# Moving a small gate product and its vector and scalar work from the middle of a projection stage to its beginning

## The reference, cut to what matters

```python
IN_SPLITS = (2 * MLSTM_HEADS * MLSTM_DQK, MLSTM_WIDTH, MLSTM_WIDTH,
    MLSTM_HEADS, MLSTM_HEADS,      # input gate, forget gate: 4 columns each
    3 * MOBA_WIDTH, MLA_Q_LORA, MLA_KV_LORA, MLA_ROPE)
...
hl = rms_norm_2(causal_block_attention(lq, lk, lv), g_mla_out)
...
mix = jnp.concatenate([hm.reshape(B, S, MLSTM_WIDTH), ha.reshape(B, S, MOBA_WIDTH),
                       hl.reshape(B, S, MLA_WIDTH)], axis=-1)
x = x + mix @ w_out
h2 = rms_norm_2(x, g_mlp_norm)
x = x + jnp.square(jax.nn.relu(h2 @ w_up)) @ w_down
```

## Time and profile before

| | us |
|---|---|
| median of 3 runs | 2105.74 |
| lowest, highest | 2096.07, 2106.62 |
| the profiled execution | 2099.57 |
| its span | 2097.4 |
| mean granted TensorE clock, share of full | 0.953 |

### The profile page before, as it was taken

How to read it: one execution, slowest core, us unless ns; L and a number is a source line. 1 busy time by engine, 2 the same in 40 slices (tenths; PEclk the granted TensorE clock), 3 DMA queues, 4 the chain that set the end, 5 groups by cost and what they waited for, 6 DMA issues and landing times.

```text
span 2097.4 us, 44494 instructions
## 1 busy us (share of the span) xinstructions
PE 1899.1 (91%) x16350; PEld 1789.6 (85%) x16350; DVE 1310.8 (62%) x1997; ACT 1145.0 (55%) x1929; POOL 960.3 (46%) x686
## 2 busy tenths in 40 slices
PE   7898788999999898788999999988799999889999
PEld 6787677999999887677999998966699998669999
DVE  2467866268943366775258973477687545768764
ACT  4644245457755655245456665664655456565544
POOL 4672017938997683015846988571200036402000
PEclk9999699999999999789999999997999999879999
DMA  5442003656665442003565665431266654204665
GB/s 191 127 126 72 1 2 113 181 149 181 186 192 168 141 131 72 21 2 96 165 173 158 186 185 157 136 100 41 81 173 198 187 165 121 76 26 142 187 192 174
DMA packets 146201, 271.51 MB, mean 129 GB/s; under 512 B 16225, under 2 KB 16482, under 8 KB 145762
## 3 DMA queue, kind: packets, MB, share of 16 engines
q1 hardware_dynamic: 144720, 265.29, 43.8%
q10 hardware_dynamic: 1298, 3.66, 0.5%
HBM read 267.84 MB, written 1.05 MB: 128 GB/s over the span
## 4 chain that ended last, share of the span: by engine, by line
PE 66%; DVE 15%; ACT 10%; POOL 5%; issue 3%; DMA 0%; ACTq 0%; DVEq 0%; SPq 0%
PE bank L655 65%; ACT arena L1281 7%; POOL ring_split L643 5%; ACT hi_ring L1281 1%; PE bank L762 1%; DVE arena L1813 1%; DVE arena L1812 1%; DVE arena L2121 1%; DVE small L2120 1%; ACT L1281 1%; DVE u L1883 1%; DVE arena L2256 0%; DMA arena<-in_masks 0%; DVE arena L2363 0%; DVE arena L2250 0%
## 5 line engine op out<-in xcount | busy, mean ns | idle before, releaser
L643 POOL TENSOR_TENSOR ring_split<-ring,hi_ring 128x512 fp32r<-128x512 f32 x682 | 960.1, 1432 | 954.5 <-ACT hi_ring L1281 943.8
L1281 ACT ACTIVATE hi_ring<-ring 128x512 fp32r<-128x512 f32 x1002 | 618.0, 630 | 519.1 <-PE bank L655 496.8
L655 PE MATMUL bank<-u_hi,hi_ring 128*128 128x256 f32 (+1 forms) x2480 | 677.5, 286 | 58.8 <-POOL ring_split L643 45.2
L655 PE MATMUL bank<-u_split,hi_ring 128*128 128x256 f32 (+1 forms) x2480 | 666.1, 281 | 0.4 <-DVE u_split L1888 0.2
L655 PE MATMUL bank<-u_hi,ring_split 128*128 128x256 f32 (+1 forms) x2480 | 666.0, 281 | 0.0
L655 PEld LDWEIGHTS bank<-u_hi,hi_ring 128*128 128x128 f32 (+1 forms) x2480 | 453.5, 188 | 73.5 <-POOL ring_split L643 51.2
L655 PEld LDWEIGHTS bank<-u_split,hi_ring 128*128 128x128 f32 (+1 forms) x2480 | 453.5, 188 | 2.7 <-DVE u_split L1888 1.0
L655 PEld LDWEIGHTS bank<-u_hi,ring_split 128*128 128x128 f32 (+1 forms) x2480 | 453.6, 188 | 1.1
L655 PE MATMUL bank<-arena 64*64 64x64 f32 (+6 forms) x3680 | 261.9, 268 | 52.6 <-ACT arena L1281 13.4
L655 PEld LDWEIGHTS bank<-arena 64*64 64x64 f32 (+3 forms) x3680 | 227.0, 165 | 93.9 <-issue 53.3
L1921 DVE TENSOR_TENSOR ring_split<-ring,hi_ring 128x512 fp32r<-128x512 f32 x320 | 215.4, 694 | 116.2 <-ACT hi_ring L1281 112.6
(11 more groups left out here) (246 smaller groups left out, 2390.0 us busy)
## 6 DMA issues: line engine op xcount, KB each, us to landing
ring<-in_stream SPq DMA_DIRECT2D x1002, 256.0 KB, 2.7
par<-in_params ACTq DMA_DIRECT2D x4, 637.0 KB, 4.9
cst<-in_cst SPq DMA_DIRECT2D x1, 1058.0 KB
h<-in_x SPq DMA_DIRECT2D x1, 1024.0 KB
out<-h ACTq DMA_DIRECT2D x3, 256.0 KB, 2.7
arena<-in_masks SPq DMA_DIRECT2D x1, 416.0 KB
out<-h ACTq DMA_DIRECT2D x2, 128.0 KB, 2.1
arena<-in_positions ACTq DMA_DIRECT2D x1, 1.0 KB
```

Source lines behind the costliest of these rows:

```text
L643: nc.gpsimd.tensor_tensor(ring_lo[:, c, :], ring[:, c, :], hi_ring[:, q % HI_RING, :].bitcast(F32), ALU.subtract).then_inc(lo_by_pool, 1)
L655: ins = nc.tensor.matmul(o, l, r, start=start, stop=stop)
L1281: return nc.scalar.activation(o, i, f, **kw)
```

## The change

The group `if` goes to the place right behind `kpe` in the bank order, in the weight stream, and in TensorE's program. On ScalarE its Abs, Exp, table load and Ln go behind the square of the latents, ahead of `aq`; a second table load, back to `natural_log_exp_and_others`, is added behind the Ln. On VectorE all ten operations go ahead of the latents' norm. The request `hi.upto("if", 0)` ahead of the root "latent qk" becomes `hi.upto("uv")`. What is computed is the same.

```diff
--- before.py
+++ after.py
@@ -101,8 +101,8 @@
 for i in range(len(MERGE)):
     SIZES1 += [(m[0], 16) for m in MERGE[i + 1:i + 2]] + [(MERGE[i][1], 8)]
 SIZES1 += [("WO", 64), ("U first", 16), ("U second", 16)] + [(f"U{i}", 16) for i in range(2, 22)] + [("D", 176)]
-SIZES2 = [("cq first", 16), ("cq second", 16), ("cq1", 8), ("kpe", 8)] + [(n, 16) for n in ("aq", "ak", "av", "qk0", "qk1")]
-SIZES2 += [("uq0", 6), ("uq1", 6), ("uk0", 2), ("uk1", 2), ("uv", 4), ("if", 8), ("mv0", 32), ("mo0", 16), ("mo1", 16)]
+SIZES2 = [("cq first", 16), ("cq second", 16), ("cq1", 8), ("kpe", 8), ("if", 8)] + [(n, 16) for n in ("aq", "ak", "av", "qk0", "qk1")]
+SIZES2 += [("uq0", 6), ("uq1", 6), ("uk0", 2), ("uk1", 2), ("uv", 4), ("mv0", 32), ("mo0", 16), ("mo1", 16)]
 SIZES2 += [("WO attention", 32), ("WO", 32), ("U first", 16), ("U second", 16)] + [(f"U{i}", 16) for i in range(2, 16)] + [("D", 256)]
 assert sum(n for _, n in SIZES1) == BLOCKS1 and sum(n for _, n in SIZES2) == BLOCKS2
 BY_VECTOR1 = {"A second", "WO", "U second"}
@@ -153,9 +153,9 @@
     gap = np.zeros((D, 28), w_in.dtype)
     uq = np.pad(w_uq.reshape(384, 4, MLA_D), ((0, 0), (0, 0), (0, P - MLA_D))).reshape(384, 4 * P)
     kv = w_ukv.reshape(256, 4, 2, 64)
-    out = [row_blocks(np.concatenate([w_in[:, 2312:2568], w_in[:, 2696:2952]], 1)), blocks(w_in[:, 2568:2696]), blocks(np.pad(w_in[:, 2952:2984], ((0, 0), (64, 32)))), blocks(w_in[:, 1544:2056]),
+    out = [row_blocks(np.concatenate([w_in[:, 2312:2568], w_in[:, 2696:2952]], 1)), blocks(w_in[:, 2568:2696]), blocks(np.pad(w_in[:, 2952:2984], ((0, 0), (64, 32)))), blocks(np.concatenate([i, gap, f], 1)), blocks(w_in[:, 1544:2056]),
            row_blocks(w_in[:, 2056:2312]), blocks(w_in[:, :512]), blocks(uq), blocks(kv[:, :, 0].reshape(256, 256)),
-           row_blocks(kv[:, :, 1].reshape(256, 256)), blocks(np.concatenate([i, gap, f], 1)), row_blocks(w_in[:, 512:1024]),
+           row_blocks(kv[:, :, 1].reshape(256, 256)), row_blocks(w_in[:, 512:1024]),
            blocks(w_in[:, 1024:1536]), blocks(w_out[512:]), blocks(w_out[:512]), row_blocks(w_up[:, :4 * P]), blocks(w_up[:, 4 * P:]), blocks(w_down)]
     assert sum(map(len, out)) == BLOCKS2
     return np.concatenate(out)
@@ -377,8 +377,8 @@
 
 
 def groups2():
-    g = ["cq0", "ckv", "cq1", "kpe", "aq", "ak", "ncq", "nckv", "av", "nq", "nk", "qk0", "qk1"]
-    g += ["uq0", "uq1", "uk0", "uk1", "uv", "rq", "rk", "nlq0", "nlq1", "nlk0", "nlk1", "if", "mv0", "mv1"]
+    g = ["cq0", "ckv", "cq1", "kpe", "if", "aq", "ak", "ncq", "nckv", "av", "nq", "nk", "qk0", "qk1"]
+    g += ["uq0", "uq1", "uk0", "uk1", "uv", "rq", "rk", "nlq0", "nlq1", "nlk0", "nlk1", "mv0", "mv1"]
     g += ["rlq0", "rlq1", "rlk0", "rlk1", "acol"]
     for r in range(len(ATT2) + 1):
         now = [ATT2[r][0]] if r < len(ATT2) else []
@@ -1109,6 +1109,14 @@
                     mm3(bank[:, 0:T], W.block(q + k), cut(u_parts, k), k == 0, k == KD - 1,
                         full="kpe" if k == KD - 1 else None)
                     W.done(q + k)
+                bank = B.open(pe, "if")
+                q = W.take("if", KD)
+                for i in range(2):
+                    for k in range(KD):
+                        mm3(bank[0:4, i * T:(i + 1) * T], [w[:, 32 * i:32 * i + 4] for w in W.block(q + k)], cut(u_parts, k), k == 0, k == KD - 1,
+                            full="if" if (i, k) == (1, KD - 1) else None)
+                        if i:
+                            W.done(q + k)
                 project("aq", 2, u_parts)
                 project("ak", 2, u_parts)
 
@@ -1153,14 +1161,6 @@
                     for g in range(2):
                         sums(f"{n}{g}", ones[0:MLA_D, 0:MLA_D], sq2[0:MLA_D, o + 2 * g:o + 2 * g + 2, :], 2, MLA_D)
 
-                bank = B.open(pe, "if")
-                q = W.take("if", KD)
-                for i in range(2):
-                    for k in range(KD):
-                        mm3(bank[0:4, i * T:(i + 1) * T], [w[:, 32 * i:32 * i + 4] for w in W.block(q + k)], cut(u_parts, k), k == 0, k == KD - 1,
-                            full="if" if (i, k) == (1, KD - 1) else None)
-                        if i:
-                            W.done(q + k)
                 project_rows(["mv0", "mv1"], u_parts, 4)
 
                 pe.wait_ge(S["lse_out"], past["lse_out"] + 1)
@@ -1663,6 +1663,14 @@
                 C.link(A(kpe[64:96, :], bank[64:96, 0:T], ACT.Copy))
                 B.release(act, "kpe")
                 C.link(A(sq2[:, 0:5, :].rearrange("p a t -> p (a t)"), cqk[:, :, :].rearrange("p a t -> p (a t)"), ACT.Square), S["latents_sq"])
+                hi.upto("if")
+                act.wait_ge(S["ls_in"], past["ls_in"] + 1)
+                fz = ifr[0:4, 4 * T:5 * T]
+                C.link(A(fz, fz, ACT.Abs))
+                C.link(A(fz, fz, ACT.Exp, scale=-1.0))
+                nc.scalar.preload_act_table_set(LN)
+                C.link(A(fz, fz, ACT.Ln, bias=1.0), S["hcol_out"])
+                nc.scalar.preload_act_table_set(LN_EXP)
                 take_raw("aq", aqk[:, 0:2, :], 2)
                 take_raw("ak", aqk[:, 2:4, :], 2)
                 C.link(A(sqa, aqk[:, :, :].rearrange("p a t -> p (a t)"), ACT.Square), S["kksq_ready"])
@@ -1687,16 +1695,9 @@
                 C.link(A(lqk[64:96, 4:8, :], spread(kpe, 4)[64:96], ACT.Copy))
                 C.link(A(sq2[0:MLA_D].rearrange("p a t -> p (a t)"), lqk[0:MLA_D].rearrange("p a t -> p (a t)"), ACT.Square), S["lse_in"])
                 take_raw("uv", lvt, 2)
-                hi.upto("if", 0)
+                hi.upto("uv")
                 rstd(C, B, ["nlq0", "nlq1", "nlk0", "nlk1"], "latent qk", 1.0 / MLA_D, rows=MLA_D, weights=hi)
 
-                hi.upto("if")
-                act.wait_ge(S["ls_in"], past["ls_in"] + 1)
-                fz = ifr[0:4, 4 * T:5 * T]
-                C.link(A(fz, fz, ACT.Abs))
-                C.link(A(fz, fz, ACT.Exp, scale=-1.0))
-                nc.scalar.preload_act_table_set(LN)
-                C.link(A(fz, fz, ACT.Ln, bias=1.0), S["hcol_out"])
                 for t in range(NT):
                     hi.upto("mv0")
                     bank = B.wait(act, f"mv{t}")
@@ -2319,6 +2320,21 @@
                 norm_parts(C, p("g_mix"), rn[:] if l else roots["gained"][0], 0, layers[0] * PIECES1 + l * PIECES2, None if l else final_scale)
                 lo.upto("cq0", 0)
 
+                bank = B.wait(dve, "if")
+                a_, f_, g_, e_, z_, w_ = (ifr[0:4, i * T:(i + 1) * T] for i in range(6))
+                C.link(V.tensor_scalar(a_, bank[0:4, 0:T], p("b_i")[0:4], None, ALU.add))
+                C.link(V.tensor_scalar(f_, bank[0:4, T:2 * T], p("b_f")[0:4], None, ALU.add))
+                B.release(dve, "if")
+                C.link(V.tensor_copy(z_, f_), S["ls_in"])
+                C.link(V.tensor_scalar(f_, f_, 0.0, None, ALU.min))
+                dve.wait_ge(S["hcol_out"], past["hcol_out"] + 1)
+                C.link(V.tensor_tensor(f_, z_, f_, ALU.subtract))
+                C.link(V.memset(w_, 1.0))
+                C.link(V.tensor_tensor_scan(z_, w_, f_, 0.0, ALU.mult, ALU.add))
+                C.link(V.tensor_tensor(a_, a_, z_, ALU.add))
+                C.link(V.tensor_tensor_scan(g_, a_, a_, 0.0, ALU.max, ALU.max))
+                C.link(V.tensor_tensor(e_, z_, g_, ALU.subtract), S["d_diff"])
+
                 refine(C, "latents", 1)
                 for i in range(5):
                     g_ = p("g_cq")[:, i:i + 1] if i < 3 else p("g_ckv")[:, i - 3:i - 2]
@@ -2348,28 +2364,12 @@
                 rope(C, B, "rk", aqk[:, 2:4, :], 2, tabs[0], tabs[1], t2)
                 dve.sem_inc(S["rope_ready"], 1)
 
-                bank = B.wait(dve, "if")
-                a_, f_, g_, e_, z_, w_ = (ifr[0:4, i * T:(i + 1) * T] for i in range(6))
-                C.link(V.tensor_scalar(a_, bank[0:4, 0:T], p("b_i")[0:4], None, ALU.add))
-                C.link(V.tensor_scalar(f_, bank[0:4, T:2 * T], p("b_f")[0:4], None, ALU.add))
-                B.release(dve, "if")
-                C.link(V.tensor_copy(z_, f_), S["ls_in"])
-                C.link(V.tensor_scalar(f_, f_, 0.0, None, ALU.min))
-
                 refine(C, "latent qk", 3, MLA_D)
                 s2f = sq2.rearrange("p a t -> p (a t)")
                 for i, n in ((0, "g_lq"), (4, "g_lk")):
                     x_ = lqk[0:MLA_D, i:i + 4, :].rearrange("p a t -> p (a t)")
                     C.link(V.scalar_tensor_tensor(x_, x_, p(n)[0:MLA_D], s2f[0:MLA_D, i * T:(i + 4) * T], ALU.mult, ALU.mult))
                 dve.sem_inc(S["lse_out"], 1)
-
-                dve.wait_ge(S["hcol_out"], past["hcol_out"] + 1)
-                C.link(V.tensor_tensor(f_, z_, f_, ALU.subtract))
-                C.link(V.memset(w_, 1.0))
-                C.link(V.tensor_tensor_scan(z_, w_, f_, 0.0, ALU.mult, ALU.add))
-                C.link(V.tensor_tensor(a_, a_, z_, ALU.add))
-                C.link(V.tensor_tensor_scan(g_, a_, a_, 0.0, ALU.max, ALU.max))
```

(1 more changed line is left out.)

## The result

The changed kernel takes 2112.27 us (median of 11 runs, 2109.61 to 2120.2) against 2101.9 (11 runs, 2095.68 to 2108.75) for the kernel before: ratio 1.0058, 95% interval 1.0041 to 1.0075, some 12 us slower by that ratio; the two medians lie 10.4 apart. The forecast was 14.4 us slower. The profiled execution has a span of 2110.3 us.

A forecast was written before the change was run, and what follows sets the result against it. TensorE, busy 91% of the span, was taken as the bound, with no room at the new place. Per stage 5.8 + 5.2 - 3.8 = 7.2 us, in all 14.4 slower: 2117 us, bounds 2105 to 2126, range 2103 to 2129.

The forecast's parts named there:

- Step 1: Behind `kpe`, TensorE's 48 moved matmuls add 5.8 us per stage to a stretch that has no idle time.
- Step 2: At `aq`, ScalarE's gate work holds up the weights and TensorE pauses; 5.2 us per stage, bounds 3.2 to 6.9.
- The short COPY: VectorE's gate COPY at the new place, clear of GpSimd's remainders, may take 0.28 us instead of 1.33.
- the clock's share: Behind TensorE's pause at `aq`, the clock runs at half rate for a while; 1.7 us lost per stage.
- Step 3: VectorE's ten gate operations run ahead of the latents' norm, where VectorE is idle; cost nothing, cover over 5 us.
- Rival C: Behind the hold, GpSimd's remainders beside VectorE's gates take 2.2 us or more instead of 1.26; 2125 us, chance 0.12.
- Step 4: At the old place, up to the first masked logits, 3.8 us gained per stage, not 7.4; TensorE becomes last.
- Rival A: VectorE's 7.4 us per stage come off the chain, the rest hides; 2088 us, chance 0.06 with other faster causes.
- B: No pause at `aq`, since pieces made ahead cover ScalarE's hold; 4.0 us slower, 2107 us, chance 0.22 with smaller pauses generally.
- D: Each of ScalarE's two gate table loads holds it as long again, 2.6 us more per stage; 2122 us, chance 0.05.

The follow-up runs named there:

- e1: Changed kernel with ScalarE making three more pieces of weights within its gate work (ahead of the `ls_in` wait, behind Exp, behind Ln); ratio to before 1.0039.
- e6: Changed kernel without the two table loads and with one more piece of weights made ahead of the `ls_in` wait; ratio to before 1.0046.
- e2: Changed kernel without the two table loads beside the gates' Ln, which uses the table already loaded; ratio to before 1.0037.
- e7: Changed kernel with two more table loads that do no work, behind the load back to `natural_log_exp_and_others`; ratio to before 1.0099.
- e3: Kernel before, nothing moved, with the gates' six VectorE operations behind the latents' scaling replaced by one memset; ratio to before 1.0007.
- e4: Against the kernel before, gates' product moved between `qk0` and `qk1`, VectorE's operations around the rotations `rq`, `rk`, ScalarE's part ahead of the root; ratio 0.9994.
- e8: Changed kernel with VectorE's last six gate operations back at their old place behind `lse_out`, the rest at the new one; ratio to before 1.0064.

## Why the prediction was right

The forecast was 14.4 us slower (2117); measured is about 12, and the marks give 12.7. The nearness owes something to luck: the half clock came behind the pause in one stage of two. By the 1.5 us that it cost there, the marks would have given about 11 with none and about 14 with both, an estimate.

**Step 1**, the product at the new place: 5.8 forecast, 5.45 found. The 5.8 came from a place where the second matmul starts 0.30 behind the first and the others 0.117 apart; here all start 0.114 apart.

**Step 2**, the hold: this was the step that decides, and it does. The pause was put at 3.2 to 4.3, taken as 3.5, and is 3.33, behind exactly 36 matmuls. The short COPY (0.28) came out, and for the reason given: in e1 and e6, where ScalarE has fed GpSimd a piece more and a remainder runs at that moment, the same COPY takes 1.20 and 1.19. e2 and e7 make the hold shorter and longer, and the pause follows to a few hundredths; in e1, with pieces made within the hold, it is gone. What was off is the clock's share, 1.7 for each stage: it was 0 in the first stage of the changed kernel and about 1.5 in the second (62.21 against 63.66). The whole step is 62.21 - 53.05 - 5.45 = 3.7 and 63.66 - 52.94 - 5.45 = 5.3, against 5.2.

**Step 3**, VectorE's ten operations at no cost: they are, since its next operation comes 15 us after them. The small pauses of 0.2 to 0.6 in `ak` in e1 and e6 are the rest of ScalarE's hold and not VectorE's doing, since GpSimd was idle ahead of each of them. Rival C has its mechanism right, far below its size: beside VectorE's gates the remainders take 1.40 each in the changed kernel (the first four behind the pause end 5.59 after they began) and 1.45 in e6 (six in 8.69), not 1.26 and not the 2.2 of the rival. In e6 that can be worth 0.6 to 0.8 us a stage, which is what its `kpe` to root is longer than before beyond the product's 5.45 and its pauses.

**Step 4**, the gain: 3.8 forecast, 3.2 and 4.0 found. That TensorE is last and no longer VectorE is what the two waits of 2.45 and 1.12 say. The two sizes differ by the half clock behind the pause of 4.17: it held for 13 matmuls of 0.63 us or more in the first stage and for 10 in the second. e3 shows that the 7.4 us on the chain were not to be had by VectorE's part alone.

Rival A is out by the sign of the result and by e3; B by the pause itself; D by e2 and e7: loads cost 1.28 each and no more. By the drain that the Trainium skill puts beside a load (ScalarE: Activation LUTs, What ACT_TABLE_LOAD costs), the two loads of e7 would have added 5.3 us to the pause, an estimate of twice its 2.66; they added 2.58. What the Trainium skill calls an exclusive lock (SBUF — State Buffer, SBUF: two separate sides), one engine blocked for the other's whole instruction, agrees with both sizes seen: a TENSOR_TENSOR on 4x256 took 1.27 to 1.34 beside GpSimd's remainders and 0.41 without them.

## What to carry to other kernels

A row on the chain of waits says that an operation was last, not by how much: ask who is second, and take the operation out without moving anything (e3) before paying for a move. A small group that uses its weights twice is a bridge over a thin supply; it belongs where the supply pauses (e4, which loses nothing against before, and gains nothing), not where the array is already full. An engine that makes another's operands, with four slots between them, must never wait in line for a third one: let it make what it may ahead of the wait.

## What the hardware showed that I had not expected

- The same pause of 3.33 us was followed by the half clock in three of four profiled stages (one of the changed kernel's, both of e8's) and by the full clock in one. The same `kpe` to root stretch cost 62.2 without and 63.4 to 63.7 with it. How long it lasts varies too: behind the same pause of 4.11 in the kernel before, 11 matmuls of 0.63 us or more in the first stage and 6 in the second. A term for it can be given only as a range.
- Whole executions of the same kernel differ by 13 us (before: 2095.68 to 2108.75), while the kernel before repeats its stretch from `kpe` to masked logits to 0.1 us. The long executions are mostly those with the lower mean granted clock: of 35 of the kernel before, measured beside e1 to e4, the 23 at 0.950 or more have a median of 2096.8, the other 12 one of 2109.6. In the profiles of before and after, the stretch from the first masked logits to VectorE's first row of line 2454 (the mLSTM branch's norm) took 65.99 and 70.05 us in the first stage, and 69.24 and 65.73 in the second, with the same instructions: the sum over both is equal to 0.6, so a comparison of one stage there would have given 4 us of either sign.
- Back-to-back table loads (e7) start 1.28 to 1.29 us apart, with nothing between them.
